# Two transformer blocks on one core: the first mixer as one interleaved list, its norm folded into its outputs

## The reference

```python
xn = rmsnorm(h, norm_mix[0])               # x * rsqrt(mean(x^2) + eps) * gain
proj = xn @ w_in                           # 1024 -> 3584
mq, mk, mv, rq, rk, rv, rg = split(proj)   # 4 heads of 128 each
mo = softmax_attention(rope(mq), rope(mk), mv)      # causal, 256 keys
ro = retention(rope(rq), rope(rk), rv)              # chunks of 128, with decay
ro = ro * rsqrt(mean(ro^2) + eps) * silu(rg)
h = h + concat(mo, ro) @ w_out
```

## Time and profile before

| | |
|---|---|
| Median of 3 runs | 2629.68 us (2628.54 to 2630.67) |
| Profiled execution | 2630.28 us, its span 2628.5 us |
| Busy PE / DVE / ACT / POOL | 97% / 75% / 46% / 4% of the span |
| Chain that ended last | PE 91%, DVE 6%, ACT 2% |
| Mean granted clock of TensorE | 0.991 |

### The profile page before, as it was taken

How to read it: one execution, slowest core, us unless ns; L and a number is a source line. 1 busy time by engine, 2 the same in 40 slices (tenths; PEclk the granted TensorE clock), 3 DMA queues, 4 the chain that set the end, 5 groups by cost and what they waited for, 6 DMA issues and landing times.

```text
span 2628.5 us, 51809 instructions
## 1 busy us (share of the span) xinstructions
PE 2560.7 (97%) x18840; PEld 2362.6 (90%) x18840; DVE 1983.2 (75%) x4076; ACT 1197.1 (46%) x1759; POOL 107.8 (4%) x65
## 2 busy tenths in 40 slices
PE   8889999999999999999999999999999999999999
PEld 7889999998899888999999998999879998778999
DVE  6678986667886788889976668976887756667774
ACT  4455554444454434455544444444335444445443
POOL 0014100000000000052000000000000000000000
PEclk9989999999999999999999999999999999999999
DMA  6335445565445555545355555355554554544554
GB/s 210 121 121 160 145 133 186 184 190 185 144 135 186 188 187 168 189 149 165 116 174 185 184 191 184 104 175 186 189 185 144 176 181 133 112 123 130 177 182 155
DMA packets 120702, 429.44 MB, mean 163 GB/s; under 512 B 14690, under 2 KB 16738, under 8 KB 120176
## 3 DMA queue, kind: packets, MB, share of 16 engines
q1 hardware_dynamic: 118464, 420.65, 50.2%
q0 software_dynamic: 2096, 6.93, 1.4%
HBM read 423.79 MB, written 3.74 MB: 163 GB/s over the span
## 4 chain that ended last, share of the span: by engine, by line
PE 91%; DVE 6%; ACT 2%; issue 1%; DMA 0%; ACTq 0%; DVEq 0%
PE acc L752 27%; PE work L465 17%; PE work L466 17%; PE work L467 17%; PE work L765 5%; DVE ring_lo L459 2%; PE acc L465 1%; PE work L970 1%; PE work L942 1%; PE work L615 1%; PE work L616 1%; PE work L617 1%; PE acc L466 1%; PE acc L467 1%; ACT ring_hi L453 1%
## 5 line engine op out<-in xcount | busy, mean ns | idle before, releaser
L459 DVE TENSOR_TENSOR ring_lo<-ring,ring_hi 128x1024 fp32r<-128x1024 f32 (+1 forms) x759 | 921.1, 1218 | 391.5 <-ACT ring_hi L453 389.3
L453 ACT ACTIVATE ring_hi<-ring 128x1024 fp32r<-128x1024 f32 (+1 forms) x799 | 833.3, 1051 | 457.8 <-PE acc L752 373.2
L465 PE MATMUL work<-normed_hi,ring_hi 128*128 128x256 f32 (+1 forms) x2960 | 854.7, 289 | 24.5 <-DVE ring_lo L459 14.9
L466 PE MATMUL work<-normed_lo,ring_hi 128*128 128x256 f32 (+1 forms) x2960 | 838.4, 283 | 0.0
L467 PE MATMUL work<-normed_hi,ring_lo 128*128 128x256 f32 (+1 forms) x2960 | 834.7, 282 | 0.0
L465 PEld LDWEIGHTS work<-normed_hi,ring_hi 128*128 128x128 f32 x2960 | 563.5, 190 | 37.4 <-DVE ring_lo L459 12.4
L752 PE MATMUL acc<-ring_hi,weighed 128*128 128x512 f32 x2048 | 584.2, 395 | 0.0
L466 PEld LDWEIGHTS work<-normed_lo,ring_hi 128*128 128x128 f32 x2960 | 562.0, 190 | 7.4
L467 PEld LDWEIGHTS work<-normed_hi,ring_lo 128*128 128x128 f32 x2960 | 560.1, 189 | 0.0
L752 PEld LDWEIGHTS acc<-ring_hi,weighed 128*128 128x128 f32 x2048 | 374.3, 188 | 80.0
L752 PE MATMUL acc<-ring_lo,weighed 128*128 128x512 f32 x1024 | 322.6, 396 | 0.0
(11 more groups left out here) (256 smaller groups left out, 2225.4 us busy)
## 6 DMA issues: line engine op xcount, KB each, us to landing
ring<-in_u SPq DMA_DIRECT2D x256, 512.0 KB, 3.5
ring<-in_v SPq DMA_DIRECT2D x256, 512.0 KB, 3.5
ring<-in_ffn_in SPq DMA_DIRECT2D x88, 512.0 KB, 3.5
ring<-in_query SPq DMA_DIRECT2D x32, 512.0 KB, 3.5
ring<-in_ffn_out SPq DMA_DIRECT2D x32, 512.0 KB, 4.0
ring<-in_even_in SPq DMA_DIRECT2D x28, 512.0 KB, 3.9
ring<-in_odd_in SPq DMA_DIRECT2D x24, 512.0 KB, 3.6
ring<-in_mix_in SPq DMA_DIRECT2D x19, 512.0 KB, 3.6
```

Of the source, the lines that this page charges most:

```text
L453: act.activation(ring_hi[:, n % RING, 0:width], ring[:, n % RING, 0:width], ACT.Copy).then_inc(hi_ready, 1)
L459: eng.tensor_tensor(ring_lo[:, n % RING, 0:width], ring[:, n % RING, 0:width], ring_hi[:, n % RING, 0:width].bitcast(F32), ALU.subtract).t ...
L465: pe.matmul(out, w_hi, hi, start=start, stop=False, **more)
L466: pe.matmul(out, w_hi, lo, start=False, stop=False, **more)
```

## The change

The stages `norm0`, `even`, `ret` and `moba` become one list, `EVEN_ITEMS`. The softmax attention's items stand between the projections, behind them the retention's. Queries and keys of a head are projected next to each other, and `EVEN_IN` puts the weight array into the same order.

The first norm is folded. The projections run on x times its gain, without the factor per token. That factor is worked out beside them (`sum`, `rstd`): ScalarE's squares are added by DVE in three halving steps, one matmul takes the mean. It then multiplies the cosine and sine tables (DVE), the gates (`raw`), and, transposed to a column (`turnr`), the values when ScalarE empties them. `raw` leaves the gate in SBUF, and Silu reads it from there.

The matmul for the rotation goes. ScalarE copies each projection three times: whole, its upper half of partitions to the lower with the sign turned, and its lower half to the upper (`qk1turn`).

The constants are loaded ahead of x, with the rotation matrix gone from them. The load of the expert keys waits for the first rotation. The attention's outputs have their own buffer (`att1_hi`, `att1_lo`). The output projection takes its parts in the order 0 to 7 where it took 0, 4, 1, 5, 2, 6, 3, 7.

Of the functions that are written anew only the new lines stand in the diff; the old ones are in the listing above.

```diff
-EVEN_ITEMS = [("proj", 0)]
-for _j in range(1, 16):
-    EVEN_ITEMS += [("proj", _j), ("rot", _j - 1)]
-EVEN_ITEMS += [("rot", 15)] + [("val", j) for j in range(4)]
+EVEN_ITEMS = [
+    ("proj", 0), ("proj", 4), ("sum", 0), ("proj", 1), ("rstd", 0), ("rot", 0), ("rot", 4), ("proj", 5), ("rot", 1), ("turnr", 0),
+    ("score", 0), ("proj", 2), ("exp", 0), ("rot", 5), ("norm", 0),
+    ("turn", 0), ("score", 1), ("proj", 6), ("exp", 1), ("rot", 2), ("norm", 1),
+    ("turn", 1), ("score", 2), ("val", 0), ("exp", 2), ("rot", 6), ("norm", 2),
+    ("mix", 0), ("turn", 2), ("score", 3), ("proj", 3), ("exp", 3), ("norm", 3), ("out", 0),
+    ("turn", 3), ("score", 4), ("proj", 7), ("exp", 4), ("rot", 3), ("norm", 4),
+    ("turn", 4), ("score", 5), ("val", 1), ("exp", 5), ("rot", 7), ("norm", 5),
+    ("mix", 1), ("turn", 5), ("score", 6), ("proj", 8), ("exp", 6), ("norm", 6), ("out", 1),
+    ("mix", 2), ("turn", 6), ("score", 7), ("proj", 12), ("exp", 7), ("rot", 8), ("norm", 7), ("out", 2),
+    ("turn", 7), ("val", 2), ("rot", 12),
+    ("mix", 3), ("inner", 0), ("proj", 9), ("decay", 0), ("out", 3),
+    ("outer", 0), ("proj", 13), ("rot", 9), ("proj", 10), ("rot", 13),
+    ("mean", 0), ("inner", 1), ("proj", 14), ("decay", 1), ("rot", 10), ("unit", 0),
+    ("outer", 1), ("proj", 11), ("rot", 14),
+    ("mean", 1), ("inner", 2), ("proj", 15), ("decay", 2), ("rot", 11), ("unit", 1), ("val", 3), ("rot", 15),
+    ("inner", 3), ("outer", 2), ("gate", 0), ("decay", 3), ("mean", 2), ("outer", 3), ("gate", 1), ("raw", 0), ("unit", 2),
+    ("mean", 3), ("gate", 2), ("raw", 1), ("silu", 0), ("silu", 1), ("tail", 0), ("unit", 3), ("tail", 1),
+    ("gate", 3), ("raw", 2), ("silu", 2), ("tail", 2), ("raw", 3), ("silu", 3), ("tail", 3)]
+EVEN_BANKS = [item for item in EVEN_ITEMS if item[0] in ("proj", "val", "gate", "turnr", "score", "turn", "mix", "inner", "outer", "mean")]
+EVEN_PROJ = [j for kind, j in EVEN_ITEMS if kind == "proj"]
+EVEN_SLOT = {"proj": lambda j: [j], "val": lambda j: [16 + 2 * j, 17 + 2 * j], "gate": lambda j: [24 + j]}
+EVEN_IN = [s for kind, j in EVEN_BANKS if kind in EVEN_SLOT for s in EVEN_SLOT[kind](j)]
...
-STAGES = [("norm0", 1), ("even", len(EVEN_ITEMS)), ("ret", len(RET_ITEMS)), ("moba", len(MOBA_ITEMS)),
-          ("evenout", K)]
+STAGES = [("even", len(EVEN_BANKS)), ("evenout", K)]
...
+sp.dma_start(const[:, :], a["const"]).then_inc(const_in, 16)
 sp.dma_start(stream[:, :, XS], a["x"]).then_inc(x_in, 16)
-sp.dma_start(const[:, :], a["const"]).then_inc(const_in, 16)
...
-            pool.wait_ge(normed_ready, K)
+            pool.wait_ge(turned_ready, 1)
...
@@ TensorE @@
 def even():
+    n = SLOT0["even"]
     for kind, j in EVEN_ITEMS:
+        w = even_bank(kind, j) if (kind, j) in EVEN_BANKS else None
+        bank = work[:, w % 4, :] if w is not None else None
+        h, t = j // NT, j % NT
         if kind == "proj":
+            project(w, n, XS, ready=first_lo if j == 0 else None)
             n += 1
+        elif kind == "gate":
+            project(w, n, XS)
+            n += 1
+        elif kind == "val":
             values(w, n, 2, [META, META + P])
             n += 2
+        elif kind == "sum":
+            pe.wait_ge(first_sum, 1)
+            pe.matmul(acc[:, 0, 0:S], cst("inv_d"), squares[:, 0, XS], start=True, stop=True).then_inc(first_done, 1)
+        elif kind == "turnr":
+            wait_bank(pe, w)
+            pe.wait_ge(first_rstd, 1)
+            for t in range(NT):
+                mm = pe.transpose(bank[:, t * P:(t + 1) * P], rstd[:, t * P:(t + 1) * P], ident)
+            mm.then_inc(bank_done[w % 4], 1)
+        elif kind == "score":
+            wait_bank(pe, w)
+            pe.wait_ge(turned_ready, EVEN_PROJ.index(HEADS + h) + 1)
+            pe.matmul(bank[:, 0:P * (t + 1)], qk1[:, h, t * P:(t + 1) * P], qk1[:, HEADS + h, 0:P * (t + 1)],
                       start=True, stop=True).then_inc(bank_done[w % 4], 1)
         elif kind == "turn":
+            wait_bank(pe, w)
+            pe.wait_ge(probs_ready, j + 1)
             for b in range(t + 1):
+                mm = pe.transpose(bank[:, b * P:(b + 1) * P], scores1[:, j % 4, b * P:(b + 1) * P], ident)
             mm.then_inc(bank_done[w % 4], 1)
+        elif kind == "mix":
+            wait_bank(pe, w)
             for t in range(NT):
+                pe.wait_ge(*freed(even_bank("turn", NT * j + t)))
+            pe.wait_ge(*freed(even_bank("val", j // 2)))
+            pe.matmul(bank[:, 0:P], val1[:, j, 0, :], prob1[:, j % 2, 0, 0:P], start=True, stop=True)
+            pe.matmul(bank[:, P:S], val1[:, j, 0, :], prob1[:, j % 2, 0, P:S], start=True, stop=False)
+            pe.matmul(bank[:, P:S], val1[:, j, 1, :], prob1[:, j % 2, 1, P:S], start=False, stop=True).then_inc(bank_done[w % 4], 1)
+        elif kind == "inner":
+            wait_bank(pe, w)
+            pe.wait_ge(turned_ready, EVEN_PROJ.index(3 * HEADS + j) + 1)
+            q, k = qk1[:, 2 * HEADS + j, :], qk1[:, 3 * HEADS + j, :]
+            pe.matmul(bank[:, 0:S], k[:, 0:P], q[:, 0:S], start=True, stop=True)
+            pe.matmul(bank[:, S:S + P], k[:, P:S], q[:, P:S], start=True, stop=True).then_inc(bank_done[w % 4], 1)
         elif kind == "outer":
+            wait_bank(pe, w)
+            pe.wait_ge(inner_ready, j + 1)
+            pe.wait_ge(*freed(even_bank("val", (HEADS + j) // 2)))
+            v = val1[:, HEADS + j, :, :]
+            pe.matmul(bank[:, 0:P], v[:, 0, :], inner1[:, j % 2, 0:P], start=True, stop=True)
+            pe.matmul(bank[:, P:S], v[:, 0, :], inner1[:, j % 2, P:S], start=True, stop=False)
+            pe.matmul(bank[:, P:S], v[:, 1, :], inner1[:, j % 2, S:S + P], start=False, stop=True).then_inc(bank_done[w % 4], 1)
+        elif kind == "mean":
+            wait_bank(pe, w)
+            pe.wait_ge(retsq_ready, j + 1)
+            pe.matmul(bank[:, 0:S], cst("inv_head"), retsq[:, j, :], start=True, stop=True).then_inc(bank_done[w % 4], 1)
...
@@ ScalarE @@
+def first_parts():
+    act.wait_ge(const_in, 16)
+    act.wait_ge(x_in, 16)
+    for k in range(K):
+        act.activation(normed_hi[:, k, XS], stream[:, k, XS], ACT.Copy, scale=gains[:, 0, k:k + 1]).then_inc(first_hi, 1)
+        if k == 3:
+            split_to(-2)
+    split_to(-1)
+    load_root()
+    for k in range(K):
+        act.activation(squares[:, k, XS], stream[:, k, XS], ACT.Square).then_inc(first_square, 1)
+
 def even():
     n = SLOT0["even"]
+    for kind, j in EVEN_ITEMS:
+        w = even_bank(kind, j) if (kind, j) in EVEN_BANKS else None
+        bank = work[:, w % 4, :] if w is not None else None
+        if kind in EVEN_SLOT:
+            n += len(EVEN_SLOT[kind](j))
             split_to(n - 1)
         if kind == "proj":
+            s = EVEN_PROJ.index(j)
+            if s >= 4:
+                act.wait_ge(turned_ready, s - 3)
+            act.wait_ge(*done(w))
+            act.activation(qk1raw[:, s % 4, :], bank[:, 0:S], ACT.Copy)
+            act.activation(qk1turn[0:HD2, s % 4, :], bank[HD2:P, 0:S], ACT.Copy, scale=-1.0)
+            act.activation(qk1turn[HD2:P, s % 4, :], bank[0:HD2, 0:S], ACT.Copy).then_inc(bank_free[w % 4], 1)
         elif kind == "val":
+            act.wait_ge(*done(w))
+            act.wait_ge(*freed(even_bank("turnr", 0)))
+            act.activation(val1[:, 2 * j:2 * j + 2, 0, :], bank[:, 0:S].rearrange("p (h d) -> p h d", h=2), ACT.Copy, scale=small[:, 2:3])
+            act.activation(val1[:, 2 * j:2 * j + 2, 1, :], bank[:, S:2 * S].rearrange("p (h d) -> p h d", h=2), ACT.Copy, scale=small[:, 3:4]).then_inc(bank_free[w % 4], 1)
+        elif kind == "rstd":
+            act.wait_ge(first_done, 1)
+            act.activation(rstd[:, 0:S], acc[:, 0, 0:S], ACT.Sqrt, bias=eps_col).then_inc(first_root, 1)
+            act.wait_ge(gains_ready, 1)
+            act.activation(root4, root4, ACT.Sqrt, bias=eps_col).then_inc(own.sem, own.up())
+            act.wait_ge(own.sem, own.n)
+        elif kind == "turnr":
+            empty(w, small[:, 2:2 + NT], bank[:, 0:S].rearrange("p (t q) -> p t q", t=NT)[:, :, 0])
+        elif kind == "exp":
+            act.wait_ge(scores_ready, j + 1)
+            row = scores1[:, j % 4, 0:P * (j % NT + 1)]
+            act.activation(row, row, ACT.Exp, bias=small[:, 8 + j % 4:9 + j % 4], accum_out=small[:, 12 + j % 4:13 + j % 4]).then_inc(exp_ready, 1)
+        elif kind == "turn":
+            h, t = j // NT, j % NT
+            if h >= 2:
+                act.wait_ge(*done(even_bank("mix", h - 2)))
+            empty(w, prob1[:, h % 2, 0:t + 1, t * P:(t + 1) * P], bank[:, 0:(t + 1) * P].rearrange("p (b q) -> p b q", q=P))
+        elif kind == "outer":
+            empty(w, ret1[:, j, :], bank[:, 0:S])
+            act.wait_ge(*freed(w))
+            act.activation(retsq[:, j, :], ret1[:, j, :], ACT.Square).then_inc(retsq_ready, 1)
+        elif kind == "mean":
+            act.wait_ge(*done(w))
 ```

(88 more changed lines are left out.)

206 lines of the change are left out of this document (27 added, 179 removed).

## The result

The changed kernel takes 2648.18 us (median of 4, 2646.69 to 2649.66) against 2630.18 (4 runs, 2628.54 to 2631.09): ratio 1.0069, interval 1.0052 to 1.0087. It is slower by 18.0 us, where 8 had been forecast (against the median of 2629.68 then on record). The profiled execution has a span of 2647.9 us, 19.4 over the one before.

The account below looks back on a forecast made before the run. TensorE, with 91% of the chain of waits, was taken to bound the kernel. From 2630.28 us, less 1.0 at full clock, plus 9 for clock falls: 2638.3, by the median's offset 2637.7; range 2621 to 2651.

Parts of the forecast that it names:

- my case: Whole kernel: pauses between projections offset the gains and clock falls add 9 us; 2637.7 us, chance 0.48.
- rival 3: Much slower: the clock falls at all 14 pauses, 22 us less 1.0; 2651 us, chance 0.14.
- the signs named beforehand: Trace signs: first projection matmul near 12.9 us, pauses before transposes, low granted clock, last output block's first eviction at 150 to 160.
- The waits: TensorE's new pauses up to the first output block, from the written order of the engines' queues: 33.6 us together.
- The rotation: Three ScalarE copies after each projection at 0.28 us each, 0.84 together; bounds 0.15 and 0.42 per half-partition copy.
- The start: First projection matmul at 12.9 us instead of 18.51, bounds 11.7 and 14.5; both transfers complete at 7.6.
- TensorE's work: Matmul work from the first projection through the first output block, including 2.3 us for initial half clock: 100.0 us.
- The clock: Half-clock spells after pauses: six counted at 1.5 us each, 9 us; bounds none and every pause.
- Rival 1: The clock holds: pauses come as summed, each followed by enough work; 2629.3 us, chance 0.24.
- rival 2: Faster: the exponential isn't held behind the projection's copies, so the mark moves 16.2 us earlier; 2613 us, chance 0.14.
- From there to the end nothing changes: After the output projection's first eviction: no change, so that eviction's shift equals the kernel's shift.
- the mark: First eviction of the output projection, at 147.83 us before; forecast at 146.8 at full clock.

Follow-up runs that it names:

- exp_first: Changed kernel with each exp item moved ahead of the projection or value item before it, TensorE's order unchanged: 2636.61 us, ratio 1.0027 to the kernel before.
- proj_last: Changed kernel with the softmax part's projection and value items moved behind the exp, rot, norm and out items that followed: 2621.67 us, 0.9968 of the kernel before.
- x_first: Changed kernel with x issued ahead of the constants again: 2645.37 us, ratio 1.0062 to the kernel before.
- keep_clock: Changed kernel with four extra fp32 matmuls of 256 columns in each of seven pauses: 2638.63 us, ratio 1.0032 to the kernel before.
- two_copies: Changed kernel with one whole copy in place of each projection's two half-partition copies, halves not exchanged: 2642.58 us, ratio 1.0044 to the kernel before.

## Why the prediction was right, and where its size was off

The time lay inside the range and the direction was the forecast one, by the forecast mechanism: pauses released by DVE's scaling behind ScalarE's copies, and falls of the clock. The size was not. The forecast was 8 us, the measured 18, and 2648.18 lies outside the 2631 to 2643 that my case was given. It is nearest to rival 3's 2651, whose condition, a fall at all 14 pauses, didn't hold. That the range held the result is owed to its width.

Of the signs named beforehand, the pauses before the transposes behind a projection (2 to 3.4 us forecast, 2.44 to 3.73 measured) and the clock under 0.9 between 28 and 95 us (0.82) came; the first matmul came 1.5 us late, the exponential 1.18 us behind the copy's start and not 0.84, and the first eviction at 165.30 lies outside 150 to 160.

**The waits.** Summed 33.6 us; the brackets sum to 34.0 (19 idle times of 0.20 us and more). Timeline of TensorE in the changed kernel, each row's idle time in its bracket:

```profile
33.09 0.74 PE L665 MATMUL work<-arena 128*128 128x128 f32 x2 [2.77 <-DVE arena L1464]
41.65 0.45 PE L671 MATMUL work<-const,arena 128*128 128x128 f32 x1 [3.73 <-DVE arena L1483]
...
66.87 0.44 PE L671 MATMUL work<-const,arena 128*128 128x128 f32 x2 [3.32 <-DVE arena_parts L1489]
74.35 0.45 PE L671 MATMUL work<-const,arena 128*128 128x128 f32 x1 [2.44 <-DVE arena L1483]
...
90.88 0.58 PE L678 MATMUL work<-arena 128*128 128x128 f32 x2 [3.14 <-DVE arena_parts L1489]
100.12 0.44 PE L671 MATMUL work<-const,arena 128*128 128x128 f32 x2 [3.31 <-DVE arena_parts L1489]
```

These are score 0 (2.9 had been summed), turn 0 (3.4), turn 3 (3.2), turn 4 (2.2), mix 2 (3.0), turn 7 (3.2). The three with a bank in the way name DVE's second pass of `out` (L1489) as releaser, as worked out from the list. The reason given for the others, the copies ahead of the exponential, was not the only one: exp_first took them away, and turns 0, 1 and 4 kept 4.2 of their 8.8 us, all six pauses 11.7 of 18.6. What stays are DVE's split, which waits for ScalarE's, and the rotation ahead of the norm; proj_last moved those as well and the pauses went. In the forecast the splits were called slack, which holds only in the order of the change.

Not everything came as listed. The pause of outer 1 (0.7 forecast) isn't there, that of turn 2 stood one item earlier, at mix 0 (1.02 against 1.3), and inner 3 (0.38) and the last mean (0.64) had not been named. The 5.2 at the output block follow from no sum that is given (four tails of three passes at 0.43 are 5.2 us, not 4.4); measured are 4.6.

A bracket also shows less than a pause costs:

```profile
37.64 0.28 PE L489 MATMUL work<-normed_hi,ring_lo 128*128 128x256 f32 x1
```

The 3.73 us before turn 0 count from the end of this matmul, 0.28 after its start. Without a pause the next one would have started 0.12 after it. So each of the 19 pauses costs 0.16 more than its bracket, 3.0 together. The forecast had counted from where TensorE is free, so the figure to set against its 33.6 is 37.0.

**The rotation.** Three copies took 1.18 us against the 0.84 taken; inside the bounds, near the upper one. These 0.34 are what most pauses had too much: counted as in the forecast turn 1 has 2.77 (2.4 summed), turn 4 2.60 (2.2), turn 3 3.48 (3.2), turn 7 3.47 (3.2).

**The start.** 14.41 against 12.9, +1.5, within the bound of 14.5. The term that was off is the 7.6 us for both transfers: with the constants issued first the pair was complete at 9.11. The edit was costed as a saving of 64 KB; against the trace of x_first it is a loss of 1.35 us, with the scatter given there.

**TensorE's work.** 100.0 had been summed to the end of the first output block, 102.8 with the second. TensorE took up the third at 167.77 us, 153.4 after 14.41. Less 34.0 for the brackets, 3.0 for what they leave out and 13.4 for the clock (next paragraph) that is 103.0: the term was right. Small fp32 matmuls between the projections do cost a gap in single places, 0.34 us in place of 0.12 in front of this one:

```profile
123.72 0.28 PE L489 MATMUL work<-normed_hi,ring_lo 128*128 128x256 f32 x1
124.06 0.46 PE L692 MATMUL work<-arena 128*128 128x128 f32 x2
```

But the kernel before has such places as well, one behind nearly every projection, where the rotation's matmul stood:

```profile
26.43 0.28 PE L467 MATMUL work<-normed_hi,ring_lo 128*128 128x256 f32 x1
26.84 0.70 PE L633 MATMUL work<-arena,const 128*128 128x256 f32 x2
```

By the sum above the interleaving costs TensorE nothing beyond the unit costs, to a few tenths of a microsecond.

**The clock.** 9 us forecast, 13.4 in the trace. It is added up from the starts of the matmuls: one of 256 columns starts every 0.21 us at half clock and every 0.12 at full. The seven low stretches between 33 and 105 us lie in this row and in that of 45 to 105 us above (0.84):

```profile
14.40:45.00 30.60, 23.06 (x140) 21.94 (x141) 20.23 (x35) 19.48 (x40) 0.70 (x1) 0.86 0.50 161
```

By the two means TensorE stood some 28 us at half clock there, a part of them idle. There were eight falls where six had been counted: one at each of the seven pauses of 2.4 us and more between 33 and 105 us (11.9 us together; the one of turn 0 alone 2.4, the others 1.5 to 1.8, near the 1.5 taken) and one in the output blocks (1.5). keep_clock agrees: the fall that it kept cost 2.1 us, counted the same way, and 13.4 less 2.1 are its 11.3. The clock did not fall after the shorter pauses between 105 and 150 us, up to 1.65, where the table shows 1.00. So the rule on small idles in the Trainium skill ("TensorE: Matmul & The Clock Gate", section "A second HAM failure mode: psum-queue depth-cycling") agrees with the trace for pauses of 2.4 us and more that come back every 7 to 17 us, and not for these. Rival 1 is refuted by the granted clock, rival 2 by the pauses; proj_last shows that rival 2's 16 us were there to be had, had the queues been ordered for it.

**"From there to the end nothing changes"** failed by 2.1 us. At the last eviction of the second layer's output projection the kernels stood 17.4 us apart (1118.38 and 1135.76), at the end 19.4. One place is seen, a pause in an untouched stage. Timeline and following stretch, the changed kernel:

```profile
2432.34 0.39 PE L487 MATMUL work<-normed_hi,ring_hi 128*128 128x256 f32 x1 [2.01 <-DVE normed_lo L1403]
...
2432.40:2435.80 3.40, 3.40 (x17) 3.40 (x18) 2.48 (x3) 1.76 (x3) 0.00 (x0) 0.54 0.56 159
```

and the kernel before, where the earlier trace rows has the pause itself:

```profile
2414.10:2417.50 3.40, 3.31 (x28) 3.31 (x29) 2.63 (x4) 1.77 (x3) 0.00 (x0) 1.00 0.53 184
```

The same pause, 2.03 and 2.01 us, left the clock at full speed in one kernel and took it to half in the other: 28 matmuls against 17 in 3.4 us. The last eviction behind it moved by 1.2 us more than the first (2415.19 to 2622.83, and 2433.33 to 2642.21). The kernels proj_last and keep_clock show the same fall behind that pause (0.61 and 0.57 over some 3.5 us), and their distance from the kernel before grew by 2.4 us each between the second eviction and the end.

The sum of the misses on the mark: start 1.5, waits 3.4, clock 4.4, work 0.2, together 9.5, where the mark moved 17.3 and 8.0 had been forecast, 9.3. With 2.1 behind it the miss is 11.4, which is 19.4 less the 8 forecast. The two large terms are the clock, by the number of falls, and the waits, by the price of the copies.

## What to carry to other kernels

Interleaving two chains on TensorE paid here only once each other engine's queue was ordered by who is waited for. An item's eviction can't start before its matmuls end, so put it behind everything that is needed to release the matmuls after them. The profile shows the mistake as an operation without an idle bracket behind one with a long idle time. Count with each pause of 2 us or more the fall of the clock that it may bring: here 13.4 us on top of 37.0.

## What the runs showed of the hardware that was not expected

- A copy of 64 partitions by 256 from PSUM cost ScalarE no less than one of 128 partitions: 0.38 us. In the sequence with half-partition copies each copy started 0.38 to 0.40 after the one before; the two whole copies of two_copies started 0.28 apart.
- With x (1 MB) issued first both transfers were complete at 7.7 to 7.8 us, with the constants first at 8.0 to 10.0 over six traces. Whether the four weight slots issued behind them are the cause was not tried.
- A pause of the same length in the same place (2.03 and 2.01 us) left the clock at 2.4 GHz in one kernel and took it to 1.2 GHz in the other, with no difference in the code of that stage. The evictions behind it moved by a further 1.2 us, for a change at the kernel's beginning.
